# Keys' rope and the transposes of the last keys, from pair 7 to pairs 1 and 2 of the projections of h

## The reference

```
h = rms_norm(x, g_pre_mix) * (1 + sc1) + sh1
mq, mk, mv, mo, mi, mf, su, sv, wq, wk, wv, gl = split_in(h @ w_in)
A: mLSTM, 4 heads x 128        (mq, mk, mv, mo, mi, mf)
B: spatial gating, 4 groups    (su, sv)
C: sliding-window attention    qs = rope(wq), ks = rope(wk), vs = wv
   new_k, new_v = ks[:, -128:], vs[:, -128:]     (prompt; all 64 rows for the sample)
merged = sum of sigmoid(gl_i) * (branch_i @ w_br_i);  x += g1 * rms_norm(merged @ w_out)
dense SwiGLU FFN, hidden 2816
```

## Time and profile before

| | |
|---|---|
| median of three executions | 2022.91 us |
| profiled execution's own time | 2023.58 us |
| its span, first to last instruction | 2021.4 us |
| PE / DVE / ACT / POOL busy | 98% / 61% / 39% / 47% |
| granted TensorE clock, mean | 0.997 of full speed |
| pair stage, first layer (PE) | 120.66 to about 286 us |
| pair stage, second layer (PE) | 1111.46 to about 1277 us |

### The profile page before, as it was taken

One profiled execution on the slowest core, in us unless ns is written; L12 is line 12 of the kernel. 1 busy time (PEld: TensorE's weight loads), 2 busy tenths in 40 slices (PEclk: granted clock), 3 DMA queues, 4 the chain that ended last, 5 costly groups with the idle time before them and its releaser, 6 DMA issues.

```text
span 2021.4 us, 39042 instructions
## 1 busy us (share of the span) xinstructions
PE 1988.2 (98%) x15901; PEld 1913.4 (95%) x15901; DVE 1240.0 (61%) x1991; ACT 781.4 (39%) x1676; POOL 949.1 (47%) x532
## 2 busy tenths in 40 slices
PE   8999999999999999999999999999999999999998
PEld 7998898999999999999999989889999999999997
DVE  5566787376647545647566667773775672747473
ACT  4234434223334343425533444442343343524253
POOL 0422244565763636363734222545749456364453
PEclk9999999999999999999999999999999999999999
DMA  9842232223351333223545223232235212233332
GB/s 357 303 147 74 58 101 100 66 73 93 96 186 43 129 128 89 85 84 100 174 163 173 69 69 85 74 101 72 77 84 177 85 53 84 84 95 89 92 93 78
DMA packets 298914, 221.41 MB, mean 110 GB/s; under 512 B 12336, under 2 KB 292464, under 8 KB 295024
## 3 DMA queue, kind: packets, MB, share of 16 engines
q1 hardware_dynamic: 294384, 215.38, 34.5%
q10 hardware_dynamic: 4352, 3.53, 0.7%
HBM read 209.37 MB, written 8.79 MB: 108 GB/s over the span
## 4 chain that ended last, share of the span: by engine, by line
PE 89%; DVE 3%; POOL 2%; DMA 2%; issue 2%; ACT 1%; SPq 0%; DVEq 0%; ACTq 0%; POOLq 0%
PE ps L1197 22%; PE ps L1298 19%; PE ps L1225 14%; PE ps L1665 10%; PE ps L1997 5%; PE ps L1318 3%; PE ps L1324 2%; PE ps L1451 1%; DMA raw<-in_w_in 1%; PE ps L1366 1%; PE ps L1897 1%; POOL hi_lo L1083 1%; PE ps L1718 1%; PE ps L1860 1%; PE ps L1733 1%
## 5 line engine op out<-in xcount | busy, mean ns | idle before, releaser
L1124 POOL TENSOR_TENSOR a_lo<-raw,a_hi 128x512 fp32r<-128x512 f32 x108 | 160.2, 1484 | 271.3 <-ACT a_hi L2694 271.3
L1080 POOL TENSOR_TENSOR hi_lo<-raw,consts 128x1024 fp32r<-128x1024 f32 x70 | 143.5, 2049 | 251.4 <-PE ps L1197 152.7
L1197 PE MATMUL ps<-h_hi,hi_lo 128*128 128x288 f32 x1216 | 218.4, 297 | 0.2 <-POOL hi_lo L1083 0.2
L1100 POOL TENSOR_TENSOR hi_lo<-raw,hi_lo 128x512 fp32r<-128x512 f32 x60 | 81.6, 1361 | 262.2 <-ACT hi_lo L2263 262.0
L1197 PEld LDWEIGHTS ps<-h_hi,hi_lo 128*128 128x128 f32 x1216 | 179.9, 189 | 4.7 <-issue 3.2
L1083 POOL TENSOR_TENSOR hi_lo<-raw,hi_lo 128x1024 fp32r<-128x1024 f32 x70 | 177.7, 2538 | 5.5
L1225 PE MATMUL ps<-yf_hi,fo_h 128*128 128x288 f32 x704 | 152.3, 298 | 1.9 <-DVE yf_lo L2869 1.9
L1225 PE MATMUL ps<-yf_hi,fo_l 128*128 128x288 f32 x704 | 151.0, 296 | 0.0
L1225 PE MATMUL ps<-yf_lo,fo_h 128*128 128x288 f32 x704 | 150.7, 296 | 0.0
L1197 PE MATMUL ps<-h_lo,hi_lo 128*128 128x288 f32 x608 | 129.9, 295 | 0.0
L1080 POOL TENSOR_TENSOR hx<-raw,consts 128x1024 fp32r<-128x1024 f32 x28 | 56.4, 2013 | 149.4 <-PE ps L1324 62.9
(11 more groups left out here) (512 smaller groups left out, 6116.4 us busy)
## 6 DMA issues: line engine op xcount, KB each, us to landing
ada<-in_w_ada SPq DMA_DIRECT2D x23, 2048.0 KB, 9.3
raw<-in_w_ffn_in SPq DMA_DIRECT2D x144, 256.0 KB, 3.1
raw<-in_w_in SPq DMA_DIRECT2D x120, 256.0 KB, 3.1
raw<-in_w_in SPq DMA_DIRECT2D x48, 512.0 KB, 3.8
raw<-in_w_ffn_out SPq DMA_DIRECT2D x32, 384.0 KB, 3.3
raw<-in_w_ffn_out SPq DMA_DIRECT2D x32, 320.0 KB, 3.1
raw<-in_w_out SPq DMA_DIRECT2D x16, 512.0 KB, 3.6
raw<-in_w_ffn_in SPq DMA_DIRECT2D x16, 512.0 KB, 3.9
```

Source lines behind the costliest of these rows:

```text
L1080: pool.tensor_tensor(hi, RAW[s][:, 0:size], ONES[:, 0:1].to_broadcast([128, size]), ALU.mult).then_inc(chunk_hi, 1)
L1100: pool.tensor_tensor(lo, RAWB[o], hi.bitcast(f32), ALU.subtract).then_inc(h_alo, 1)
L1124: pool.tensor_tensor(lo[:, :], RAWB[o], hi[:, :].bitcast(f32), ALU.subtract).then_inc(s_alo, 1)
L1197: m = pe.matmul(o[:, h, :], a[:, k, c0:c0 + 128], mv(k, h), start=(k == 0 and begins), stop=(k == nk - 1 and a is wl))
```

## The change

PE's `rope(4)` goes from pair 7 (after p5) to pair 1 (between p7 and p3). `key_window` goes from pair 7 (after rope(1)) to pair 2 (between p6 and p2). DVE's three instructions of rope(4) go from pair 7 (after its work for p6) to the end of its work for pair 1; its wait for the sin and cos tables goes ahead of pair 0. ACT's two copies to KOUT go from pair 8 to pair 2; the outputs stay in pair 8. NROWS leaves KOUT, which now holds the keys from pair 2 on, for a tile of TS. The two DMAs to KB stay where ACT issues them, with one more wait (s2 of pair 5 has been read). MIX, and with it the PSUM alternation, follows. The helper functions only change their place in the file.

```diff
-MIX = ["hc", "hr", "gt3", "kt0", "vt0", "vt1", "cm0", "kt1", "cm1", "vt2", "kt2", "cm2", "vt3", "kt3", "cm3"]
+MIX = ["hc", "hr", "gt3", "kt0", "vt0", "vt1", "cm0", "kt1", "r4", "cm1", "vt2", "kt2", "ko", "cm2", "vt3", "kt3", "cm3"]
-MIX += _b(3)[1] + ["r4", "r0", "r1", "ko", "r2", "r3", "svt0", "svt1", "sc0"]
+MIX += _b(3)[1] + ["r0", "r1", "r2", "r3", "svt0", "svt1", "sc0"]
-        NROWS = KOUT[0:4, :, :]
+        NROWS = TS[0:4, 1, 0:256].rearrange("p (j c) -> p j c", j=2)
 (PE)
                 key_transposes(1)
-                h_products(1, "p7", "p3")
+                h_products(1, "p7")
+                rope(4)
+                h_products(1, "p3")
                 key_transposes(2)
-                h_products(2, "p6", "p2")
+                h_products(2, "p6")
+                key_window()
+                h_products(2, "p2")
...
-                h_products(7, "p5")
-                rope(4)
-                h_products(7, "p6", "p2")
+                h_products(7, "p5", "p6", "p2")
                 rope(0)
                 h_products(7, "p7", "p3")
                 rope(1)
-                key_window()
                 h_products(7, "p4")
 (ACT, pair 2)
                 after_p2(2)
+                act.wait_ge(done_by("ko"), done(l, "ko"))
+                act.activation(KOUT[:, 0, :], unit(l, "ko")[:, 0:128], ACT.Copy)
+                act.activation(KOUT[0:64, 1, :], unit(l, "ko")[0:64, 128:256], ACT.Copy).then_inc(unit_of(l, "ko"), 1)
 (ACT, pair 7, ahead of the DMAs to KB)
+                act.wait_ge(h_slo, 4 * (l * NHP + 5) + 2)
                 act.wait_ge(rope_ready, nth(rope_ready, l, 0))
 (ACT, pair 8)
-                act.wait_ge(done_by("ko"), done(l, "ko"))
-                act.activation(KOUT[:, 0, :], unit(l, "ko")[:, 0:128], ACT.Copy)
-                act.activation(KOUT[0:64, 1, :], unit(l, "ko")[0:64, 128:256], ACT.Copy).then_inc(unit_of(l, "ko"), 1)
 (DVE)
                 new_state(1)
                 after_p4(1)
+                rope(4)
                 after_p1(2)
...
                 after_p6(7)
-                rope(4)
                 rope_sine(0)
```

More of the change, by code:

```diff
@@ L1828, in key_window @@
                     pe.transpose(unit(l, "ko")[0:64, 128:256], KA[:, SEQ:T], IDN).then_inc(done_by("ko"), 1)
+                h_products(0, "p1", "p5", "p6")
+                row_columns()
+                h_products(0, "p2", "p7")
+                key_transposes(0)
+                h_products(0, "p3", "p4")
+                h_products(1, "p1")
+                to_tokens("vt0", "v", 0)
+                h_products(1, "p5")
+                to_tokens("vt1", "v", 1)
+                h_products(1, "p6")
+                state(0)
+                h_products(1, "p2")
+                key_transposes(1)
+                h_products(1, "p7")
+                rope(4)
+                h_products(1, "p3")
+                state(1)
+                h_products(1, "p4")
+                h_products(2, "p1")
+                to_tokens("vt2", "v", 2)
+                h_products(2, "p5")
+                key_transposes(2)
+                h_products(2, "p6")
+                key_window()
+                h_products(2, "p2")
+                state(2)
+                h_products(2, "p7")
+                to_tokens("vt3", "v", 3)
+                key_transposes(3)
+                h_products(2, "p3", "p4")
+                state(3)
+                for h in range(4):
+                    row_spread(h)
+                    h_products(3 + h, "p1")
+                    if h:
+                        back(h - 1)
+                    h_products(3 + h, "p5", "p6")
+                    scores(h, 0)
+                    h_products(3 + h, "p2")
+                    scores(h, 1)
+                    h_products(3 + h, "p7")
+                    outputs(h)
+                    h_products(3 + h, "p3", "p4")
                 h_products(7, "p1")
                 back(3)
-                h_products(7, "p5")
-                rope(4)
-                h_products(7, "p6", "p2")
+                h_products(7, "p5", "p6", "p2")
                 rope(0)
@@ L3315, in _, with rope_sine, rope_sum, rope @@
                     modulation_done(1, 3)
+                if l == 0:
+                    dve.wait_ge(tables_loaded, 16)
+                else:
+                    dve.wait_ge(tables_loaded, 48)
+                def rope_sine(i):
+                    nm = f"r{i}"
+                    if i < 4:
+                        dve.wait_ge(rope_ready, nth(rope_ready, l, i))
+                    dve.wait_ge(done_by(nm), done(l, nm))
+                    tt(split2(TS[:, 1, :]), halves(l, nm), split2(K_["sin"]), ALU.mult).then_inc(unit_of(l, nm), 1)
+                def rope_sum(i):
+                    nm = f"r{i}"
+                    raw = KA[:, 0:T] if i == 4 else WQ[:, i, :]
+                    if i == 4:
+                        dve.wait_ge(unit_of(l, "wk"), read(l, "wk"))
+                    else:
+                        h_tile_done(dve, l, "wq", i)
+                        dve.wait_ge(rope_ready, nth(rope_ready, l, i))
+                    tt(TS[:, 0, :], raw, K_["cos"], ALU.mult).then_inc(dve_step, step())
+                    dve.wait_ge(dve_step, step.all())
+                    dve.wait_ge(unit_of(l, nm), read(l, nm))
+                    tt(raw, TS[:, 0, :], TS[:, 1, :], ALU.add).then_inc(rope_ready, 1)
+                def rope(i):
+                    rope_sine(i)
+                    rope_sum(i)
                 after_p1(0)
@@ L3434, in _ @@
                 gate_head(3)
[L3436 to L3466, removed]
                 after_p5(7)
```

## The result

The kernel after takes 2028.03 us (median of 14 runs, 2026.31 to 2033.24), the kernel before on the same occasion 2023.71 us (14 runs, 2020.15 to 2027.50): ratio 1.0025, 95% interval 1.0017 to 1.0033. The forecast was 2023.7 us and no change within 0.2%; the change costs about 0.25%, outside the predicted range. The profiled execution of the kernel after took 2033.24 us and was the slowest of the 14. I compare it with the 2023.58 us of before stage by stage, so that what is only its own shows.

The account below looks back on a forecast made before the run. PE, busy 98%, was taken as the bound. Per layer 1.19 − 1.19 + 0.22 + 0.2 = +0.42 us, twice +0.84, on the profiled 2023.58 gave 2024.4; the median, 0.67 lower, 2023.7 us; range 2020.0 to 2026.2.

Parts of the forecast that it names:

- What bounds the place: Pairs 8 and 9: PE's stalls, about 2.4 us over both layers, follow DVE's chain, which waits for a22's load.
- the relief of DVE in pair 7: Some 3.9 us of DVE work leaves pair 7, with no price on PE, since DVE idles 0.96 us and awaits the load.
- over 3 us: Sign: DVE's idleness ahead of s1 of pair 8 should grow to over 3 us from 0.96.
- What comes in pairs 1 and 2: PE takes on 0.97 and 0.22 us per layer; s3 of pair 2 slips about 1.0 us, without reaching PE.
- the collision with POOL: Pair 2: POOL's a12 part, 1.28 us, falls on DVE's last moved instruction; included in s3's 1.0 us slip.
- Add c, what a22's load loses by the earlier DMAs to KB: Pair 8's a22 load: c is its delay per layer, taken as 0.2 us, bounds 0 and 0.9.
- The rule that I laid beside c: DMA engines alternate between queue rows, so two DMAs queued behind the LayerNorm loads cost a22 near 0; sum +0.44 us.
- So the chain moves up by 0.97: Pair 7 to p5 of pair 9: chain gains only rope(4)'s 0.97 us; key_window's 0.22 becomes stall per layer.
- Rival 2: DMAs to KB get in front of a22, delaying the chain to p5 of pair 9: +2.2 us, 2025.1 us; chance 0.10.
- The later stalls: Sign: rope(2) to the second matmul behind it takes 1.4 to 1.7 us instead of 1.21; behind rope(3) as before.

Follow-up runs that it names:

- e1: Kernel after, with the two DMAs to KB issued behind ACT's work for p4 of pair 7 instead of right behind the LayerNorm loads: 2023.62 us, ratio 1.0000.
- e7: Kernel after, with the first DMA to KB left early and the second issued behind p4 of pair 7: 2027.04 us, ratio 1.0017.
- e9: Kernel before, ropes untouched, two extra same-size copies right behind the LayerNorm loads and the real ones behind p4 of pair 7: 2027.73 us, ratio 1.0023.
- e10: Kernel after, copies of the keys still early, with the two LayerNorm loads moved behind p4 of pair 7: 2021.69 us, ratio 0.9988.
- e4: Kernel after, with the two DMAs to KB in pair 6 behind p2 and the LayerNorm loads behind p4 of pair 7: 2021.53 us, ratio 0.9989.
- e3: Kernel before, with only the two LayerNorm loads moved behind p4 of pair 7: 2021.93 us, ratio 0.9990.
- e5: Kernel after, with twenty matmuls into unread columns ahead of the last matmul of p1 of pair 8: 2029.86 us, ratio 1.0036.
- e11: Kernel after, unchanged, run once more for a second profile: 2030.58 us (one run).

## Why the prediction was wrong, by its steps

- **What bounds the place: right.** p5 hangs on DVE, DVE on a22's load, and the relief of DVE in pair 7 was worth nothing. DVE now idles for 4.79 us there ("over 3 us").
- **What comes in pairs 1 and 2: right.** No wait of PE appears there in either layer. DVE's three instructions ran at 0.75, 0.75 and 0.76 us from 150.96 on, and the collision with POOL that I put on the last one did not happen (POOL's part started at 152.69, the last of the three at 152.41); s3 of pair 2 took 1.59 instead of 1.25, unnoticed by PE.
- **"Add c, what a22's load loses by the earlier DMAs to KB": this step failed.** I took 0.2 with an upper end of 0.9; it measured 6.3 − 4.4 = 1.9 us, and e1, e7 and e9 show that the copies in the load's flight are the cause. The upper end came from a rate (1.3 us for 512 KB), and "they were in flight together before the change as well" was false comfort: issued at 254.72 and 255.28 into a load that was to land at 256.74, the copies' packets began at 255.90, when the load had 0.5 us of packets left (its last ended at 256.40).
- **The rule that I laid beside c: its condition did not hold.** The Trainium skill, page "DMA: Bandwidth & Descriptors", section "Queues, rings and completion order", has each DMA engine go round-robin over the rows that have work, packet by packet; from it I took "c near 0" as long as the layer norm's two loads last. They did not last. In the trace the load is 512 packets of 512 B, the two loads 256 of 2,048 B, the copies 128 of 2,816 B. When the load's first packet starts in the kernel after (256.18), 219 of those 256 have started, and 85 packets of the copies start between its first and its last, against 40 before.
- **What the 1.9 us consist of.** From issue to first packet it is 2.06 us before and 1.96 after, from there to the end of the last packet 2.00 and 3.38, from there to landing 0.34 and 0.97. The count of turns does not explain the middle part: ACT's queue starts 133 packets in it before and 122 after. But more of them are the copies', at about 200 ns each, where one of the layer norm's took 89 before, and the load's own packets take 46 ns each instead of 28. Why they do, and why the landing lags, stays open.
- **"So the chain moves up by 0.97": failed too, with a smaller price.** The load's issue was to come 0.22 us later in the stage and came 1.57 later, in e1 and e10 as well (133.16, 133.24). rope(4) had covered ACT's copy of p1. With `h_products(7, "p5", "p6", "p2")` in one call PE now waits for that copy ahead of p5's last matmul (249.23, 0.46 us later than at the usual pitch). So p5 ends late, on top of the 1.19 us of moved work that now stand ahead of it, DVE's sum behind it starts at 249.74 instead of 247.57, and ACT, which works in order, reaches a22's hi part at 251.87 instead of 250.33 (0.31 of it is the later start of the stage, 0.22 was expected). Removed PE work between two chained products was cover for another engine. Alone this costs little: e1 carries all of it at 1.0000. By the profiles of e4 and e3 (165.31 against 164.06 us for the first stage) the whole move would cost 1.25 us a layer with the load left alone; their medians do not show it.
- **Rival 2 named the mechanism**: the copies get in front of a22, and it decides early. Its price, +2.2 us, was half of the measured 4.3. The place was wrong, in it as in the forecast: both looked for the stall ahead of p7 of pair 8 and p5 of pair 9, and neither asked for the lead at p5 of pair 8, the first product behind s1. That lead was 0.18 us, and PE lost 2.65 there.
- **The later stalls** did not grow to 1.4 to 1.7 us behind rope(2) but vanished (269.84 to 270.59 there, 277.17 to 277.92 at rope(3)): a stall of 2.65 us ahead gives DVE its lead back, while PE ran at half clock.
- **Still open:** both profiled executions of the kernel after lose about 7 us in the two stages (the 1.7 taken off), the median of the runs 4.3; the profiled executions of e7 and e9 lose 4.5 and 3.0 in the stages, and each was the fastest of its 12. That the stall varies from run to run with how the queues meet would fit, but is not shown; I have no profile of a median run.

The best versions found are e10, e4 and e3, all 0.1% below the kernel before, with intervals that reach nearly to 1. What they share is that the LayerNorm's loads are kept out of the flight of pair 8's weights; where the keys' rope stands makes no difference between their medians.

## What to carry to other kernels

A step that is moved takes its DMAs along, and one that becomes ready sooner is issued sooner: lay the packets of both, as the trace times them, over whatever transfer the critical chain waits for, and ask how much lead the first consumer of that transfer has (0.18 us here). A small filler between two chained pieces may be the cover for a copy on another engine; look for who finishes during it before it is taken away. And a lower clock behind a long wait is not by itself lost time: see whether the engine would have waited anyway.

## What was not expected of the hardware

- 256 KB took 2.7 us with nothing beside it, 3.0 behind two SBUF copies issued 0.7 us and more ahead, 3.7 beside 512 KB of loads, 5.3 with one copy of 176 KB added and 6.3 with two; 5.9 to 6.7 in the two layers of e5, e9 and e11. What the two copies cost it beside nothing else, in its flight, no run here measures.
- The copies, 2.8 us by themselves, took 6.1 in that crowd. From 258 to 260 us the DMA engines were busy for 0.76 of the time, yet moved little (kernel after, columns as above, 118 GB/s):

```profile
258.00:260.00 2.00, 2.00 (x18) 2.00 (x17) 0.00 (x0) 0.00 (x0) 0.00 (x0) 1.00 0.76 118
```
